# Later chunks of seven norms read an operand already scaled by the norm, and more weight chunks take wide products

## The chip, the cores and the metric

The kernel runs on 1 core of one Trainium2 chip. The metric is the device time of one execution in microseconds (us), the median of the runs shown. The profile is one further execution of the same program. The core has five engines that run side by side: TensorE (PE; its weight loads are shown apart as PEld), VectorE (DVE), ScalarE (ACT), GpSimd (POOL) and SyncE (SP), which issues the loads of the weights. Each engine takes its own instructions strictly in the order of the program, and they wait for one another on semaphores.

## The reference, cut to what matters

The program is four transformer blocks on one sequence of 256 tokens and width 1024: two of a first kind, then two layers of a second kind.

```python
# first kind, twice (the mixer differs)
h = h + mixer(rms_norm(h, mix_norm_g[l]))
h = h + conv_ffn(rms_norm(h, ffn_norm_g[l]), ...)     # conv of the 2*3072 columns, u * gelu(g), down

# second kind, two layers
h = swiglu(rms_norm_2(x, ffn1_pre[l]), w_gate_up, w_down)        # 2*2816 columns
x = x + 0.5 * rms_norm_2(h, ffn1_post[l])
z = rms_norm_2(x, mix_pre[l]) @ w_in                             # b_g, c_g, v, p, gates
y_a = (b_g * causal_depthwise_conv(c_g * v, conv_w)) @ w_conv_out
y_p = pool_mixer(p, ...) @ w_pool_out                            # trailing means over 2, 4, 8, 16
x = x + rms_norm_2((g_a * y_a + g_p * y_p) @ w_o, mix_post[l])
h = swiglu(rms_norm_2(x, ffn2_pre[l]), ...)                      # like the first
```

A norm is `x * 1/rms(x) * gain`. All matrices are float32.

## The kernel before

The activations stand with the 1024 channels in 8 tiles of 128 partitions and the 256 tokens along the free side. The weights, 313 chunks of 1 MB (128 partitions x 16 blocks of 128 columns), are streamed once. A chunk is two output tiles (256 output channels) for 8 input tiles.

**Split products.** Every operand is split in two float32r parts, a high one and the rest. ACT makes the high part of a chunk (`w_hi`, L234), DVE the rest (`w_lo`, L243, a subtraction of 128x2048), and PE sums high x high, high x low and low x high. There are 3 buffers for raw chunks (`RAWS`) and 4 for split ones (`RING`): while DVE and ACT treat chunk n, ACT splits chunk n + 4 and DVE makes the rest of chunk n + 3. SP issues the load of chunk n + 3 when the rest of chunk n is made.

**Narrow and wide chunks.** `multiply` (L261 to L263) takes 48 matmuls for a chunk: 8 input tiles x 2 output tiles x 3 products of 256 columns. Its two output tiles share one PSUM bank. `multiply_wide` (L277, L282) puts the high and the low part of the activation side by side into one matmul of 512 columns, which leaves 32: 16 of 512 columns and 16 of 256. Its output tiles take a whole bank each, and their right halves (the high x low product) must be added to the left ones. ACT copies the right halves out (L781) and DVE adds them (L324). The rotation through the PSUM banks has `BANKS` = 4. A narrow chunk takes one of them and a wide chunk two. PE may start a chunk when DVE has taken the last user of its banks (semaphore `pair_taken`): a narrow chunk waits for the take of the chunk 4 before it, a wide one among wide ones for the take of the chunk 2 before it.

Before the change the wide chunks are the down projections and, of the gated expansions `upA` and `upB` of the second kind, the chunks from the 6th (`NARROW` = 5) on, 17 in each.

**Norms.** The mean of squares that a norm needs comes late. So the chunks after a norm multiply `x * gain` (the tile `x_split`, split by L420 and L425), and DVE multiplies each result by the reciprocal `inv_rms` when it takes it from PSUM (`take_scaled`, L330; for a wide chunk it is a second operation, L327). `inverse_spread` (L368) makes that reciprocal at the second chunk. After a post norm of the second kind, x itself has still to be divided by that norm's rms: DVE makes the reciprocal in `unroot_dve` (L382) and POOL multiplies x by it in place, 4 operations in `residual_pool` (L393).

**The stages around the change.** `up_dve`, `up_act` and `up_pool` treat the results of an expansion, chunk by chunk. In `up0` and `up1` (24 chunks each, first kind) DVE takes a chunk, makes a rest (L243), and does 4 convolution taps (L831), and POOL does two operations (L881, L887). In `upA` and `upB` (22 chunks) the activation needs no taps. `hybrid_dve`, `hybrid_act` and `pool_means` treat the mixer's input projection: 4 chunks `bg`, 4 `pool_in`, 8 `cv`, 8 `gates`. In `bg` chunk 3 DVE runs `unroot_dve` for the norm before. In `pool_in` chunk g DVE takes the chunk, makes a rest (L243), waits for ACT's high part of the pooled difference g - 1, subtracts (L1753), and sums the windows (L1781, L1782). POOL makes the mean and the difference of chunk g from these windows (L1745, L1748), ACT rounds the difference (L1368), and so on for the next g. POOL's first mean stands in its queue behind its 4 operations on x.

## Time and profile before

| what | us |
|---|---|
| median of 3 runs | 1861.85 (1861.85 to 1862.13) |
| the profiled execution: time | 1861.95 |
| the profiled execution: span | 1860.1 |
| PE busy, of the span | 1822.5 |
| DVE busy | 1436.2 |
| ACT busy | 972.5 |
| POOL busy | 204.1 |

The span runs from the first instruction to the end of the last; the rest of the time lies around it. Matmuls are pipelined, so the busy time of a group of them adds overlapping instructions only once, while a single matmul's duration is far longer than the distance from its start to the next one's. The distance between starts is what a matmul costs in a full stream.

### The profile page before, as it was taken

The page shows a single profiled execution, that of the slowest core. Times are in us where ns is not written, and L with a number is a line of the kernel's source. Part 1 is how long each engine was busy: PE and PEld are TensorE (multiplying, and loading weights), DVE is VectorE, ACT ScalarE, POOL GpSimd, SP SyncE. Part 2 cuts the span into 40 slices and gives each one's busy share as a digit, 9 for nine tenths or more (in the row PEclk, how much of TensorE's full clock was granted, in tenths as well). Part 3 has the DMA queues.
Part 4 walks back from the last instruction along what each step waited for, and adds up shares of the span by engine and source line. Part 5 has one row for each costly group of instructions (what it writes and reads, how often), then busy time and mean ns, then how long its engine had stood idle before and what let it go on. Part 6 is the DMA issues. An engine that isn't in the chain of part 4 may idle for free.

```text
span 1860.1 us, 31793 instructions
## 1 busy us (share of the span) xinstructions
PE 1822.5 (98%) x13284; PEld 1720.6 (92%) x13284; DVE 1436.2 (77%) x1707; ACT 972.5 (52%) x1174; POOL 204.1 (11%) x160
## 2 busy tenths in 40 slices
PE   7999999999999999999999999999999999999997
PEld 7889999999999998899999998889888999999887
DVE  7987996598998578758875797759775896578774
ACT  6356665385765455544453555545553445445542
POOL 2001321000432030002200010001000320001000
PEclk9999999999999999999999999999999999999999
DMA  7324555434555545564454455554555445445551
GB/s 291 131 105 159 184 183 201 182 137 181 182 204 181 204 159 183 204 221 146 164 199 175 159 188 197 192 193 167 196 204 204 159 174 191 157 161 205 199 207 67
DMA packets 46789, 334.67 MB, mean 180 GB/s; under 512 B 5184, under 2 KB 5568, under 8 KB 6464
## 3 DMA queue, kind: packets, MB, share of 16 engines
q1 hardware_dynamic: 46512, 332.20, 49.3%
q8 instruction: 105, 1.72, 0.4%
q0 software_dynamic: 144, 0.52, 0.1%
q14 instruction: 28, 0.23, 0.0%
HBM read 331.65 MB, written 1.05 MB: 179 GB/s over the span
## 4 chain that ended last, share of the span: by engine, by line
PE 82%; DVE 10%; ACT 3%; POOL 2%; DMA 1%; issue 1%; SPq 0%; DVEq 0%; ACTq 0%
PE psum L277 24%; PE psum L282 12%; PE psum L261 11%; PE psum L263 11%; PE psum L262 11%; PE psum L303 6%; DVE w_lo L243 4%; PE psum L310 3%; POOL scratch L1748 1%; DMA w_raw<-stream_in 1%; POOL x_resid L393 1%; ACT w_hi L234 1%; POOL scratch L1745 1%; DVE scratch L330 1%; PE psum L599 1%
## 5 line engine op out<-in xcount | busy, mean ns | idle before, releaser
L234 ACT ACTIVATE w_hi<-w_raw 128x2048 fp32r<-128x2048 f32 x313 | 597.3, 1913 | 416.3 <-PE psum L263 157.6
L243 DVE TENSOR_TENSOR w_lo<-w_raw,w_hi 128x2048 fp32r<-128x2048 f32 x313 | 724.1, 2316 | 37.8 <-ACT w_hi L234 37.7
L261 PE MATMUL psum<-x_split,w_hi 128*128 128x256 f32 x1896 | 541.0, 285 | 13.9 <-DVE x_split L425 10.5
L262 PE MATMUL psum<-x_split,w_hi 128*128 128x256 f32 x1896 | 537.0, 283 | 0.0
L263 PE MATMUL psum<-x_split,w_lo 128*128 128x256 f32 x1896 | 537.0, 283 | 0.0
L261 PEld LDWEIGHTS psum<-x_split,w_hi 128*128 128x128 f32 x1896 | 364.4, 192 | 15.4 <-issue 14.8
L262 PEld LDWEIGHTS psum<-x_split,w_hi 128*128 128x128 f32 x1896 | 364.5, 192 | 0.5
L263 PEld LDWEIGHTS psum<-x_split,w_lo 128*128 128x128 f32 x1896 | 364.4, 192 | 0.0
L277 PE MATMUL psum<-x_split,w_hi 128*128 128x512 f32 x1088 | 341.7, 395 | 0.0
L277 PE MATMUL psum<-h_split,w_hi 128*128 128x512 f32 x816 | 256.3, 395 | 0.0
L282 PEld LDWEIGHTS psum<-x_split,w_lo 128*128 128x128 f32 x1088 | 204.4, 188 | 48.3
L282 PE MATMUL psum<-x_split,w_lo 128*128 128x256 f32 x1088 | 213.7, 278 | 0.0
L282 PEld LDWEIGHTS psum<-h_split,w_lo 128*128 128x128 f32 x816 | 153.3, 188 | 36.2
L277 PEld LDWEIGHTS psum<-x_split,w_hi 128*128 128x128 f32 x1088 | 165.6, 189 | 0.0
L282 PE MATMUL psum<-h_split,w_lo 128*128 128x256 f32 x816 | 160.3, 278 | 0.0
L393 POOL TENSOR_TENSOR x_resid<-x_resid,squares 128x512 f32<-128x512 f32 x24 | 45.4, 1923 | 902.6 <-DVE squares L382 902.5
L261 PE MATMUL psum<-h_split,w_hi 128*128 128x256 f32 x480 | 136.1, 283 | 1.3 <-ACT scratch L1298 0.7
L262 PE MATMUL psum<-h_split,w_hi 128*128 128x256 f32 x480 | 135.8, 283 | 0.0
L263 PE MATMUL psum<-h_split,w_lo 128*128 128x256 f32 x480 | 135.8, 283 | 0.0
L330 DVE TENSOR_TENSOR scratch<-psum,inv_rms 128x512 f32<-128x512 f32 x137 | 92.7, 683 | 43.3 <-PE psum L263 42.8
L277 PEld LDWEIGHTS psum<-h_split,w_hi 128*128 128x128 f32 x816 | 124.2, 189 | 0.0
L781 ACT ACTIVATE scratch<-psum 128x512 f32<-128x512 f32 x68 | 40.6, 598 | 158.5 <-PE psum L282 158.5
(249 smaller groups left out, 2412.3 us busy)
## 6 DMA issues: line engine op xcount, KB each, us to landing
w_raw<-stream_in SPq DMA_DIRECT2D x313, 1024.0 KB, 4.8
x_resid<-x_in SPq DMA_DIRECT2D x1, 1024.0 KB, 7.1
y_out<-x_resid SPq DMA_DIRECT2D x4, 256.0 KB, 2.5
scratch<-mask_in SPq DMA_DIRECT2D x1, 768.0 KB, 11.1
scratch<-ev_in SPq DMA_DIRECT2D x1, 512.0 KB, 9.7
scratch<-inv_in POOLq DMA_DIRECT2D x1, 512.0 KB, 6.6
params<-par_in SPq DMA_DIRECT2D x1, 247.0 KB, 7.3
matrices<-mat_in SPq DMA_DIRECT2D x1, 192.0 KB, 8.9
```

The costliest lines, as they stand in the source:

```text
L234: act.activation(w_hi[:, n % RING, :], raw[:, n % RAWS, :], ACT.Copy).then_inc(hi_ready, 1)
L243: dve.tensor_tensor(w_lo[:, n % RING, :], raw[:, n % RAWS, :], w_hi[:, n % RING, :].bitcast(F32), ALU.subtract).then_inc(lo_ready, 1)
L261: pe.matmul(dst, w_hi[:, c.slot, b:b + P], src[:, k0 + k, 0, :], start=opens, stop=False)
L262: pe.matmul(dst, w_hi[:, c.slot, b:b + P], src[:, k0 + k, 1, :], start=False, stop=False)
L263: done = pe.matmul(dst, w_lo[:, c.slot, b:b + P], src[:, k0 + k, 0, :], start=False, stop=last and k == nk - 1 and m == len(tiles_) - 1)
L277: pe.matmul(ps[:, bank_, :], w_hi[:, c.slot, b:b + P], src[:, k0 + k, :, :].rearrange("p a t -> p (a t)"), start=first and k == 0, stop=False)
L282: done = pe.matmul(tile(bank_, 0), w_lo[:, c.slot, b:b + P], src[:, k0 + k, 0, :], start=False, stop=last and k == nk - 1)
L303: pe.matmul(tile(c.bank, m), w[:, c.slot, b:b + P], src[:, k0 + k, 0, :], start=k == 0 and m == 0 and w is w_hi, stop=False)
L310: done = pe.matmul(tile(c.bank, m), w_hi[:, c.slot, b:b + P], src[:, k0 + k, 1, :], start=False, stop=k == nk - 1 and m == 1)
L330: dve.tensor_tensor(dst, bank(c.bank, tiles), rinv[:, :].unsqueeze(1).to_broadcast([P, tiles, T]), ALU.mult).then_inc(pair_taken, 1)
L393: pool.tensor_tensor(x[:, 2 * g:2 * g + 2, :], x[:, 2 * g:2 * g + 2, :], UNRMS.unsqueeze(1).to_broadcast([P, 2, T]), ALU.mult).then_inc(*t ...
L781: act.activation(S(ACC + 2 * c.slot, 2), ps[:, c.bank:c.bank + 2, T:2 * T], ACT.Copy)\
```

## The change

1. `WIDE` and `SCALED` say for each stage from which chunk on it is wide, and from which it is scaled. Wide are now also: `up0` and `up1` from chunk 7 (17 chunks each), `pool_in` chunk 3, all 8 `cv` and all 8 `gates` chunks of both layers. `upB` is wide from chunk 6 and not from 5. `upA` stays.
2. A scaled chunk (all the newly wide ones, and `upA` and `upB` from chunk 7) multiplies another operand, x times the gain times the reciprocal. DVE makes it with 8 operations (`scale_dve`), ACT rounds it with 4 (`scaled_hi`) and DVE makes the rest with 4 (`scaled_lo`). Its result needs no second multiplication. There are eight of these operands in an execution.
3. In an expansion, DVE makes the operand behind chunks 2 and 3 and the rests behind chunks 4 and 5, each the last of its chunk. In the mixer, it makes the operand behind `bg` chunk 2 and the rests behind `bg` chunk 3.
4. `unroot_dve` stands behind these: in `upA` and `upB` at chunk 5 and not 3, in the mixer still at `bg` chunk 3, but after the rests.
5. PE waits, in a scaled chunk, for rest k // 2 + 1 before input tile k.

```diff
-WIDE = ("upA", "upB")
+WIDE = {"up0": 7, "up1": 7, "upA": 5, "upB": 6, "pool_in": 3, "cv": 0, "gates": 0}
+SCALED = {"up0": 7, "up1": 7, "upA": 7, "upB": 7, "pool_in": 3, "cv": 0, "gates": 0}
...
         def take_scaled(dve, c, dst, tiles=2):
             dve.wait_ge(chunk_done, c.number + 1)
             if c.wide:
-                dve.wait_ge(up_right, wide_count(c))
-                dve.tensor_tensor(dst, ps[:, c.bank:c.bank + 2, 0:T], S(ACC + 2 * c.slot, 2),
+                dve.wait_ge(up_right, WIDE_COUNT[c.number])
+                dve.tensor_tensor(dst, ps[:, c.bank:c.bank + 2, 0:T], right_halves(c),
                                   ALU.add).then_inc(pair_taken, 2)
+                if c.scaled:
+                    return
...
+        def copy_right(act, c):
+            act.activation(right_halves(c), ps[:, c.bank:c.bank + 2, T:2 * T], ACT.Copy).then_inc(up_right, 1)
...
+        def scale_dve(dve, tr, phase, gain, ks):
+            for k in ks:
+                dve.scalar_tensor_tensor(out=scaled_words(phase)[:, k, 1, :], in0=x[:, k, :],
+                                         scalar=gain[:, k:k + 1], in1=rinv[:, :],
+                                         op0=ALU.mult, op1=ALU.mult).then_inc(*tr["xn"].one())
+
+        def scaled_hi(act, tr, phase, gs, l):
+            for g in gs:
+                act.wait_ge(*tr["xn"].count(2 * g + 2, l))
+                act.activation(scaled_operand(phase)[:, 2 * g:2 * g + 2, 0, :],
+                               scaled_words(phase)[:, 2 * g:2 * g + 2, 1, :], ACT.Copy)\
+                   .then_inc(*tr["xhi"].one())
+
+        def scaled_lo(dve, tr, phase, gs, l):
+            for g in gs:
+                dve.wait_ge(*tr["xhi"].count(g + 1, l))
+                both = scaled_operand(phase)[:, 2 * g:2 * g + 2, :, :]
+                dve.tensor_tensor(both[:, :, 1, :], scaled_words(phase)[:, 2 * g:2 * g + 2, 1, :],
+                                  both[:, :, 0, :].bitcast(F32), ALU.subtract).then_inc(*tr["xlo"].one())
...
+            if c.scaled:
+                multiply_wide(pe, c, (c.bank, c.bank + 1), scaled_operand(c.phase), 0, KT, True, True,
+                              lambda k: tr["xlo"].count(k // 2 + 1, c.layer), hooks=hooks)
...
# up_act
+                if phase in SCALED and at in (3, 4):
+                    scaled_hi(act, pre, phase, (0, 1) if at == 3 else (2, 3), l)
...
# up_dve
-                    if at == 3 and post is not None:
-                        unroot_dve(dve, *post)
+                if phase in SCALED and at in (2, 3):
+                    scale_dve(dve, pre, phase, gain, range(0, 4) if at == 2 else range(4, 8))
+                if phase in SCALED and at in (4, 5):
+                    scaled_lo(dve, pre, phase, (0, 1) if at == 4 else (2, 3), l)
+                if at == 5 and post is not None:
+                    unroot_dve(dve, *post)
...
# hybrid_act
                 refill_hi(act, c)
+                if g == 2:
+                    scaled_hi(act, N["normM"], "pool_in", G4, l)
...
                 act.wait_ge(chunk_done, c.number + 1)
+                if c.wide:
+                    copy_right(act, c)
                 refill_hi(act, c)
...
# hybrid_dve
                 refill_lo(dve, c)
+                if g == 2:
+                    scale_dve(dve, N["normM"], "pool_in", gains2("mpre", l), range(KT))
                 if g == 3:
+                    scaled_lo(dve, N["normM"], "pool_in", G4, l)
                     unroot_dve(dve, PN["postA"], l)
```

## Rows read from the trace of the kernel before

**Rows 1.** The page: busy time of each engine.

```profile
PE 1822.5 (98%) x13284; PEld 1720.6 (92%) x13284; DVE 1436.2 (77%) x1707; ACT 972.5 (52%) x1174; POOL 204.1 (11%) x160
```

**Rows 2.** Stages up0, up1: length, busy PE, PEld, DVE, ACT, POOL, clock.

```profile
165.40:291.40 126.00, 126.00 (x1051) 125.96 (x1051) 121.78 (x139) 82.10 (x115) 42.01 (x43) 1.00 0.53 187
459.60:585.60 126.00, 126.00 (x1050) 125.96 (x1050) 121.33 (x139) 83.80 (x116) 43.82 (x43) 1.00 0.51 183
```

**Rows 3.** Timeline of PE: first matmuls of two successive chunks, narrow, then wide.

```profile
1529.81 0.28 PE L261 MATMUL psum<-x_split,w_hi 128*128 128x256 f32 x1
...
1535.57 0.28 PE L261 MATMUL psum<-x_split,w_hi 128*128 128x256 f32 x1
...
779.80 0.40 PE L277 MATMUL psum<-h_split,w_hi 128*128 128x512 f32 x1
...
785.38 0.40 PE L277 MATMUL psum<-h_split,w_hi 128*128 128x512 f32 x1
```

**Rows 4.** Timeline of PE in layer 0's mixer: cv chunk 3 starts.

```profile
907.65 0.36 PE L261 MATMUL psum<-x_split,w_hi 128*128 128x256 f32 x1 [1.24 <-DVE w_lo L243]
```

**Rows 5.** Timeline of DVE in layer 0's mixer, bg chunk 2 to cv chunk 1.

```profile
847.05 3.25 DVE L425 SCALAR_TENSOR_TENSOR x_split<-x_resid,params,x_split 128x256 fp32r<-128x256 f32 x8
...
869.59 1.74 DVE L382 RECIPROCAL squares<-squares 128x256 f32<-128x256 f32 x1
...
884.40 0.69 DVE L1753 TENSOR_TENSOR h_split<-scratch,h_split 128x512 fp32r<-128x512 f32 x1 [3.21 <-ACT h_split L1368]
...
907.43 1.50 DVE L1814 TENSOR_TENSOR scratch<-scratch 128x256 f32<-128x256 f32 x1
909.35 0.69 DVE L1753 TENSOR_TENSOR h_split<-scratch,h_split 128x512 fp32r<-128x512 f32 x1 [0.42 <-ACT h_split L1368]
909.96 0.69 DVE L330 TENSOR_TENSOR scratch<-psum,inv_rms 128x512 f32<-128x512 f32 x1
...
914.47 0.69 DVE L330 TENSOR_TENSOR scratch<-psum,inv_rms 128x512 f32<-128x512 f32 x1
```

**Rows 6.** Timeline of POOL in the same stretch.

```profile
871.41 7.63 POOL L393 TENSOR_TENSOR x_resid<-x_resid,squares 128x512 f32<-128x512 f32 x4 [169.51 <-DVE squares L382]
878.99 3.35 POOL L1745 TENSOR_TENSOR scratch<-scratch 128x512 f32<-128x512 f32 x1
882.41 1.29 POOL L1748 TENSOR_TENSOR scratch<-scratch 128x512 f32<-128x512 f32 x1
```

**Rows 7.** Timeline of DVE: four rests of 128x512.

```profile
428.36 2.49 DVE L1721 TENSOR_TENSOR h_split<-scratch,h_split 128x512 fp32r<-128x512 f32 x4
```

**Rows 8.** Timeline of DVE: takes of chunks 3 and 5 in up0, of 3 in up1.

```profile
178.60 0.68 DVE L330 TENSOR_TENSOR scratch<-psum,inv_rms 128x512 f32<-128x512 f32 x1
179.21 2.28 DVE L243 TENSOR_TENSOR w_lo<-w_raw,w_hi 128x2048 fp32r<-128x2048 f32 x1
182.86 2.65 DVE L831 SCALAR_TENSOR_TENSOR scratch<-scratch,params 128x255 f32<-128x255 f32 x4 [1.38 <-ACT scratch L773]
...
190.79 0.68 DVE L330 TENSOR_TENSOR scratch<-psum,inv_rms 128x512 f32<-128x512 f32 x1
...
473.98 0.68 DVE L330 TENSOR_TENSOR scratch<-psum,inv_rms 128x512 f32<-128x512 f32 x1
```

**Rows 9.** Timeline of PE: chunk 7 of up0 and of up1 starts.

```profile
193.18 0.28 PE L261 MATMUL psum<-x_split,w_hi 128*128 128x256 f32 x1
...
487.27 0.28 PE L261 MATMUL psum<-x_split,w_hi 128*128 128x256 f32 x1
```

**Rows 10.** ACT's copies of right halves, all of them.

```profile
L781 ACT ACTIVATE scratch<-psum 128x512 f32<-128x512 f32 x68 | 40.6, 598 | 158.5 <-PE psum L282 158.5
```

**Rows 11.** Loads of chunks: count, size, us from issue to landing.

```profile
w_raw<-stream_in SPq DMA_DIRECT2D x313, 1024.0 KB, 4.8
```

**Rows 12.** The clock: two of PE's first matmuls, and a stretch behind its last.

```profile
12.98 0.41 PE L263 MATMUL psum<-x_split,w_lo 128*128 128x256 f32 x1
13.19 0.41 PE L261 MATMUL psum<-x_split,w_hi 128*128 128x256 f32 x1
...
1853.00:1856.00 3.00, 0.00 (x0) 0.00 (x0) 2.93 (x7) 0.00 (x0) 0.00 (x0) 0.55 0.46 175
```

More of the change, by code:

```diff
@@ L98 @@
 EV_GK, EV_Q = 2, 3
-PRE, ACC, GEL, HID, HB = 0, 8, 16, 20, 24
+PRE, ACC, GEL, HID, HB, XN = 0, 8, 16, 20, 24, 24
+HYBRID = ("bg", "pool_in", "cv", "gates")
+SCALED_NORMS = ["ffnnorm0", "ffnnorm1", "normA", "normM", "normB"]
 YA, PIN, GA, GP, PRE2, ACC2, UU, INV = 0, 8, 16, 24, 32, 38, 41, 44
@@ L157, in __init__ @@
         self.slot = self.number % RING
-        self.wide = phase in WIDE and n >= NARROW
-        self.event = E0[phase] + n + layer * LAYER_EVENTS + (n - NARROW if self.wide else 0)
+        self.wide = phase in WIDE and n >= WIDE[phase]
+        self.scaled = phase in SCALED and n >= SCALED[phase]
+        self.event = E0[phase] + n + layer * LAYER_EVENTS + (n - WIDE[phase] if self.wide else 0)
         self.bank = self.event % BANKS
+        assert not self.wide or self.bank % 2 == 0, phase
         self.last = self.event + 1 if self.wide else self.event
@@ L167, in chunks @@
     return [Chunk(phase, n, layer) for n in range(done, count)]
+WIDE_COUNT, UNSCALED_COUNT = {}, {}
+_w, _u = 0, 0
+for _layer, _stages in [(0, FIRST)] + [(_l, LAYER) for _l in range(LAYERS2)]:
+    for _name, _nc, _ in _stages:
+        for _n in range(_nc):
+            _chunk = Chunk(_name, _n, _layer)
+            _w += _chunk.wide
+            _u += _chunk.wide and not _chunk.scaled
+            WIDE_COUNT[_chunk.number], UNSCALED_COUNT[_chunk.number] = _w, _u
 def program(nc, x_in, stream, par1_in, par2_in, ev_const, mask_const, mats, inv_in, out):
@@ L743, in up_tracks @@
             return {k: Signal(sem(f"{name}_{k}_ready"), 2 * m if k == "taps" else m) for k in names}
-        def wide_count(c):
-            return (WIDE.index(c.phase) + 2 * c.layer) * (FF2 - NARROW) + c.n - NARROW + 1
         def scaled(c):
-            if c.wide:
-                return up_scaled, wide_count(c)
-            return taken(c.event)
+            if c.wide and not c.scaled:
+                return up_scaled, UNSCALED_COUNT[c.number]
+            return taken(c.last)
         def up_act(act, phase, n, tr, func, conv, pre, l, final=None):
@@ L769, in taps @@
                 w, b = conv
-                act.wait_ge(*taken(c.event))
+                act.wait_ge(*taken(c.last))
                 for t in range(2):
@@ L1410, in hybrid_act @@
                 act.wait_ge(chunk_done, c.number + 1)
+                copy_right(act, c)
                 refill_hi(act, c)
-                act.wait_ge(*taken(c.event))
+                act.wait_ge(*taken(c.last))
                 for t, dst in enumerate((GA, GP)):
@@ L1775, in hybrid_dve @@
                     pooled_lo(g - 1)
-                dve.wait_ge(*taken(c.event))
+                dve.wait_ge(*taken(c.last))
                 src = S(PIN + 2 * g, 2)
```

62 lines of the change are left out of this document (40 added, 22 removed).

## The prediction

> **What bounds the kernel now.** I read the page first: PE is busy for 98% of the span, DVE for 77%, ACT for half, POOL for a tenth [rows 1]. So a shorter stream of matmuls is worth its whole length, but only where nothing else comes last. The busy time of stages says where DVE is close behind: in up0 it is busy for 121.78 of 126.00 us and in up1 for 121.33 of 126.00, with PE never idle [rows 2]. The waits of PE and its timeline then show the one stall that comes in both mixers: cv chunk 3 starts at 907.65 after 1.24 us of idling that a weight rest of DVE ends [rows 4]; it is the same at 1507.08 in layer 1. The timelines of DVE and POOL there show what makes DVE late. DVE's reciprocal at 869.59 lets POOL work on x from 871.41 for 7.63 us; then POOL makes the first mean and difference, and DVE gets them at 884.40 after 3.21 us of idling [rows 5, 6]. From there DVE, POOL and ACT hand a loop on: DVE's four subtractions L1753 run from 884.40 to 909.35, and the rest of cv chunk 3 is done at 907.43, between the last two [rows 5]. That is when PE goes on. So in the mixer the start of that reciprocal sets PE's time, and there is no slack in it.
>
> **What a wide chunk gives.** A narrow chunk takes 1535.57 - 1529.81 = 5.76 us, a wide one 785.38 - 779.80 = 5.58 us [rows 3], though both stream the same number of columns. That is 0.18 us for each. Newly wide are 17 + 17 chunks of up0 and up1 and 1 + 8 + 8 in each mixer, 34; each upB loses one. Net 66 chunks, 11.9 us at most.
>
> The Trainium skill (TensorE: Matmul & The Clock Gate, "Back-to-back issue gap") speaks against the change: it gives a start-to-start gap of columns / 2.4 plus about 2.5 ns. By it a chunk is 48 x 109.2 ns = 5.24 us narrow and 16 x (215.8 + 109.2) ns = 5.20 us wide, and 66 chunks an estimated 2.6 us and not 11.9. The rows show 120 ns for each narrow matmul, so I go by them.
>
> **What each newly wide chunk costs elsewhere.** ACT copies the right halves, 0.60 us [rows 10]; with 82 to 84 us busy in 126 [rows 2] it has room for 17 of them (10 us). DVE's take is an addition in place of a multiplication, taken as equal. The 60 chunks of upA and upB that are now scaled lose DVE's second operation. DVE has slack there, so this gives nothing. The cost that counts is that only two wide chunks fit into the PSUM banks, so DVE's take of the chunk before the last must be done when a chunk starts; until now it was the fourth before.
>
> **The new operand.** Eight operations of DVE of 128x256 with a scalar: 3.2 us, 0.40 each, as the eight of the same form that split x took 3.25 [rows 5]. Four rests of 128x512: 2.4 us, 0.60 each, as the four of that form took 2.49, of which the last's end overlaps the next operation [rows 7]. ACT's four rounds run beside. Together DVE gets 5.6 us of work, eight times. Where that is hidden it costs nothing:
>
> *upA, upB.* DVE has no taps there. I followed the work through chunks 2 to 5: the last two rests end about 1.5 us or more before PE needs them in chunk 7. The later unroot_dve starts POOL's work on x two chunks later, and the next reader of x comes only after the down projection. Cost 0; POOL slows DVE while it works, at worst some 0.7 us in upA of layer 1. Each upB is 0.18 slower, 0.4 in all.
>
> *up0.* DVE's take of chunk 3 stands at 178.60. Four scalings come before it (1.6 us), and DVE's idle 1.38 us at 182.86, a wait for ACT, absorbs them or, if ACT is also pushed back, doesn't. Four more scalings (1.6) and two rests (1.2) move the take of chunk 5 from 190.79 [rows 8] to 190.79 + 1.6 - 1.4 + 1.6 + 1.2 = 193.8, or 195.2. Behind it are the take (0.6), a weight rest (2.2), taps (2.6) [rows 8] and only then the third rest of the operand (0.6): ready at 199.8 to 201.2. PE starts chunk 7 at 193.18 [rows 9]; with 4 input tiles behind it (2.8 us) it needs that rest at 196.0. It waits 3.8 to 5.2 us. I take 4.4.
>
> *up1.* The same, but DVE stands at 473.98 where it stood at 178.60, 295.4 later [rows 8], and PE at 487.27 where it was at 193.18, only 294.1 later [rows 9]. It waits 1.3 longer, 5.1 to 6.5 us; I take 5.7.
>
> After this DVE gains on PE: its chunk is 0.6 + 2.2 + 2.6 = 5.4 us against 5.58. So one stall in each. Sum of up0 and up1: 4.4 + 5.7 - 34 x 0.18 = +4.0 us.
>
> *The mixer.* The eight scalings and four rests all stand between bg chunk 2 and the reciprocal, and DVE works without a pause there. The reciprocal moves from 869.59 to 875.2, POOL's start from 871.41 to 877.0 [rows 5, 6]. POOL's 7.63 us then end at 884.6, inside a weight rest that slows both (as at 878.99, 3.35 us for an operation that takes 1.29 alone) [rows 6]. DVE's first subtraction goes from 884.40 to 889.3 or, with the last operation on x caught too, 890.1. The loop from there took 24.95 us to the fourth (884.40 to 909.35) and is the same. So the fourth is at 914.3 to 915.1, and the take of cv chunk 1, which stands right behind it, ends 1.2 us later, 915.5 to 916.3. Until now nobody waited for that take. Now cv chunk 3 needs its banks: it starts at 915.5 to 916.3 and not at 907.65 [rows 4], 7.9 to 8.7 us later. I take 8.3. PE meets the same hold at cv chunks 0, 1 and 2, with some 3 us of idling each, all contained in this figure, as are the shorter pool_in 3 to cv 2. Left to gain are 13 wide chunks (cv 3 to 7, gates), 2.3 us; DVE's 914.47 - 909.96 = 4.5 us for a cv chunk, or 4.9 with a rest of the convolution in it, is short of 5.58. Each mixer +6.0, both +12.0.
>
> *Loads.* SP issues the load of chunk n + 3 behind the rest of chunk n, so loads move with DVE. A load lands in 4.8 us [rows 11], and it has three chunks of 5.6 less ACT's split and DVE's rest; nothing waits for it.
>
> **The clock.** PE's first matmuls come 0.21 us apart where the later ones come 0.12 apart, and behind the last matmul, at 1850.8, the granted clock falls from 1.00 (2.4 GHz) to a mean of 0.55 in the stretch 1853 to 1856 [rows 12], so the lower level is 0.5 (1.2 GHz). From the first matmul at 10.5 to the rise at about 13.4 us are 14 matmuls at 0.09 more each, 1.3 us. No gap inside the kernel is longer than 1.7 us and none lowers the clock, so the new gaps of 3 to 6 us are outside what the trace shows: 0 to 1.3 us each, eight of them. I take one, for the longest. The Trainium skill (the same page, "What's actually happening") says that an idle array is put back to half the clock. It says nothing about the price here.
>
> **The sum.** +4.0 + 12.0 + 0.4 + 1.3 = +17.7 us. From 1861.95, the time of the profiled execution (0.1 above the median of the runs): 1879.6 us, 0.95% slower. Its own range: up stages 2.8 to 5.6, mixers 11.2 to 12.8, clock 0 to 5, upA up to 0.7: 1876 to 1886.
>
> **The rivals.**
> - *Only the mixers stall.* If the rests of the operand come in time in up0 and up1 (DVE finds 5 us of pauses more than I see), these gain 6.1: 1861.95 + 12.0 + 0.4 - 6.1 = 1868.3. For: with PE at 98%, DVE's idle time is hard to place. Against: 4.2 us of it in 126, and the need comes at chunk 7.
> - *Faster: DVE's extra work is hidden everywhere.* That needs a reciprocal in bg chunk 3 on which PE's stall doesn't hang, and a DVE that catches up before chunk 7. Then 66 x 0.18 come off: 1850. It decides from the point where all added stalls are together below 11.9 us. For: DVE idles 3.21 us at 884.40. Against: that idling is a wait for the very loop that the reciprocal starts.
> - *Only up0 and up1 stall.* The mixer's stalls stay as now and it gains 17 x 0.18 twice: 1861.95 + 4.0 + 0.4 + 1.3 - 6.1 = 1861.6, no change.
> - *The clock falls in every gap.* Seven more times 1.3: 1888.7. Against: in the mixer PE waits for POOL anyway, and a slower chunk is partly hidden by the next wait.
> - *The old wait stays the last.* If the two banks don't bind, cv chunk 3 waits only for its weight rest, 4.9 to 5.7 later: 1879.6 - 6 = 1873.6. It lies in the range.
>
> **Chances.** My sum with its near variants (the last rival too) 0.73; only mixers 0.10; hidden everywhere 0.08; only up stages 0.04; clock everywhere 0.05. The range 1867 to 1888 leaves out the second and third of these other cases and the top of the last. A measurement of this kernel can tell about 0.2% (3.7 us) from no change. Faster 0.09, within 0.2% 0.04, slower 0.87.
>
> **What would show it.** In the profile after: fewer matmuls by 66 x 16 = 1056; chunks 5.58 us apart in up0, up1, cv and gates; in both mixers L382 some 5.6 us later after the start of its stage; PE waits of about 3 us at cv 0, 1, 2 that end with DVE's take, not with w_lo; cv chunk 3 some 8 us late; in up0 and up1 one wait each inside chunk 7, released by a DVE rest of the scaled operand; no stall in upA and upB. If PE's waits in up0 and up1 are missing, the forecast is 8 to 10 us too high; if L382 isn't late or cv 3 doesn't follow it, 12 to 16 too high, and the sign can turn.

## The result, and the profile after

The changed kernel takes 1889.7 us (median of 4 runs, 1887.06 to 1892.69) against 1861.99 us of the kernel before (4 runs, 1861.85 to 1863.18). The ratio is 1.0148, with a 95% interval of 1.013 to 1.0165: 1.5% slower. The forecast was 1879.6 us with a range of 1867 to 1888. The sign and the places were right, the loss was 28.8 us (profiled executions, 1861.95 to 1890.76) in place of 17.7, and the time lies 1.7 us above the range. Of all runs shown below one, of the kernel that is wide only where DVE keeps up, took 2528.9 us at a mean granted clock of 0.655; its median and ratio leave it out. The title counts seven norms; the scaled operands are eight in an execution, as the change says.

The page of the changed kernel begins with its span and the busy time of each engine, to be read against [rows 1]:

```profile
span 1889.0 us, 29813 instructions
PE 1826.4 (97%) x12228; PEld 1673.2 (89%) x12228; DVE 1439.2 (76%) x1741; ACT 1020.4 (54%) x1272; POOL 206.4 (11%) x160
```

There are 13284 - 12228 = 1056 fewer matmuls, as forecast, and yet PE is busy for 3.9 us longer: a part of the new matmuls ran slowly. The waits of PE hold three entries of several us that the kernel before did not have, all on lines of the wide chunk. Each gives the line that waits, the engine and line waited for, the us in total, how many times, and the longest:

```profile
PE psum L304 <- DVE scaled_split L399: 11.0, 4, 3.4
PE psum L304 <- DVE scratch L351: 9.9, 7, 3.2
PE psum L304 <- DVE scratch L359: 7.6, 2, 3.8
```

L399 is the rest of the scaled operand, L351 and L359 are DVE's takes of wide and of narrow chunks. Lines have moved: L243 of before is L270 (rest of a weight), L330 is L359, L324 is L351, L382 is L454 (the reciprocal), L393 is L465 (POOL on x), L1745 is L1828, L1753 is L1836.

The timeline of PE shows where these waits lie. Its columns are start and duration in us, the instruction, and in brackets the idling before it with what ended it. First come the two in up0, then three of cv in layer 0:

```profile
194.56 0.71 PE L304 MATMUL psum<-scaled_split,w_hi 128*128 128x512 f32 x2 [1.44 <-DVE scaled_split L399]
201.00 1.22 PE L304 MATMUL psum<-scaled_split,w_hi 128*128 128x512 f32 x2 [3.42 <-DVE scaled_split L399]
...
903.39 1.22 PE L304 MATMUL psum<-h_split,w_hi 128*128 128x512 f32 x2 [3.83 <-DVE scratch L359]
911.68 0.73 PE L304 MATMUL psum<-h_split,w_hi 128*128 128x512 f32 x2 [1.14 <-DVE scratch L351]
920.77 1.22 PE L304 MATMUL psum<-h_split,w_hi 128*128 128x512 f32 x2 [3.23 <-DVE scratch L351]
```

Two such matmuls take 0.71 to 0.73 us behind a short wait and 1.22 us behind a wait of over 3 us. The windows of those stretches (start and end, length, busy PE, PEld, DVE, ACT, POOL, granted clock, share of the DMA engines, GB/s) say why:

```profile
199.70:206.50 6.80, 5.50 (x17) 4.72 (x18) 6.80 (x10) 1.71 (x4) 2.14 (x2) 0.50 0.47 163
500.10:506.90 6.80, 5.83 (x18) 4.96 (x19) 6.80 (x9) 2.01 (x5) 2.14 (x2) 0.50 0.48 175
902.90:906.30 3.40, 2.90 (x9) 2.52 (x10) 3.34 (x2) 0.00 (x0) 3.32 (x2) 0.50 0.00 0
919.90:926.70 6.80, 5.93 (x18) 5.06 (x19) 6.38 (x7) 1.92 (x3) 4.48 (x2) 0.50 0.26 87
```

In each the granted clock is 0.50, the 1.2 GHz level. In these four it begins while PE is still idle: from 199.7 where PE goes on at 201.00, from 902.9 where it goes on at 903.39. There are two more, of 3.4 us each, from 1513.8 and 1530.9, which begin 0.6 and 0.3 us after PE goes on. The kernel before has none from its rise at about 13.5 us until PE's work is over.

The table gives the length of each stage, worked out as the difference between the ends of the last matmuls of successive stages in the timeline of PE.

| stage | before, us | after, us | difference |
|---|---|---|---|
| up0 | 139.34 | 144.05 | +4.71 |
| up1 | 138.66 | 144.76 | +6.10 |
| pool_in, each layer | 23.04 | 22.85 | -0.19 |
| cv of layer 0, of layer 1 | 47.55, 47.53 | 57.64, 56.45 | +10.09, +8.92 |
| gates, each layer | 46.08 | 44.59 | -1.49 |
| upA of layer 0, of layer 1 | 124.39, 127.62 | 124.39, 128.99 | 0, +1.37 |
| upB of layer 0, of layer 1 | 128.02, 128.09 | 128.70, 128.66 | +0.68, +0.57 |
| the first stage | | | -0.2 |
| all others | | | 0 |

These add up to 28.9 us, the whole difference within rounding.

DVE in layer 0's mixer, to be read against [rows 5], from the new scalings to the fourth subtraction:

```profile
877.41 3.25 DVE L382 SCALAR_TENSOR_TENSOR h_spare<-x_resid,params,inv_rms 128x256 f32<-128x256 f32 x8
...
883.38 2.49 DVE L399 TENSOR_TENSOR h_split<-h_spare,h_split 128x512 fp32r<-128x512 f32 x4
885.79 1.75 DVE L454 RECIPROCAL squares<-squares 128x256 f32<-128x256 f32 x1
...
900.59 0.69 DVE L1836 TENSOR_TENSOR h_split<-scratch,h_split 128x512 fp32r<-128x512 f32 x1 [4.46 <-ACT h_split L1445]
...
920.03 0.68 DVE L351 TENSOR_TENSOR scratch<-psum,scratch 128x512 f32<-128x512 f32 x1
...
925.44 0.69 DVE L1836 TENSOR_TENSOR h_split<-scratch,h_split 128x512 fp32r<-128x512 f32 x1 [0.41 <-ACT h_split L1445]
```

And POOL in the same stretch, against [rows 6]:

```profile
887.61 9.66 POOL L465 TENSOR_TENSOR x_resid<-x_resid,squares 128x512 f32<-128x512 f32 x4 [159.30 <-DVE squares L454]
897.23 1.29 POOL L1828 TENSOR_TENSOR scratch<-scratch 128x512 f32<-128x512 f32 x1
```

Compare distances from the end of the stage bg, which is at 866.10 before and 876.72 after. The reciprocal is 3.49 us behind it before and 9.07 after. The first subtraction is at 18.30 and 23.87, the fourth at 43.25 and 48.72. So all three are 5.5 to 5.6 us later, about the length of the inserted work (3.25 + 2.49 less overlaps), and nothing between absorbs it. POOL's part is longer on x and shorter on the first mean, 7.63 + 3.35 before and 9.66 + 1.29 after: 10.98 and 10.95 us, the same.

### The profile page after: what moved, and what is told of

Its sections match the earlier page's. It is cut to its first block, busy times and chain, and to the rows that moved or that the text cites. A ratio compares the mean times of both kernels' runs of the same rounds, so it can differ in the third digit from the quotient of the medians.

```text
span 1889.0 us, 29813 instructions
## 1 busy us (share of the span) xinstructions
PE 1826.4 (97%) x12228; PEld 1673.2 (89%) x12228; DVE 1439.2 (76%) x1741; ACT 1020.4 (54%) x1272; POOL 206.4 (11%) x160
## 4 chain that ended last, share of the span: by engine, by line
PE 73%; DVE 19%; ACT 3%; POOL 3%; issue 1%; DMA 1%; SPq 0%; DVEq 0%; ACTq 0%; POOLq 0%
PE psum L304 34%; PE psum L309 17%; DVE w_lo L270 6%; PE psum L330 6%; PE psum L288 3%; PE psum L290 3%; PE psum L289 3%; PE psum L337 3%; DVE scratch L359 1%; POOL x_resid L465 1%; DVE scratch L904 1%; POOL scratch L1831 1%; ACT w_hi L261 1%; DVE scratch L382 1%; DVE inv_rms L440 1%
## 5 line engine op out<-in xcount | busy, mean ns | idle before, releaser
L270 DVE TENSOR_TENSOR w_lo<-w_raw,w_hi 128x2048 fp32r<-128x2048 f32 x313 | 726.2, 2322 | 37.7 <-ACT w_hi L261 37.6
L304 PE MATMUL psum<-scaled_split,w_hi 128*128 128x512 f32 x1504 | 476.9, 399 | 12.4 <-DVE scaled_split L399 11.0
L304 PE MATMUL psum<-h_split,w_hi 128*128 128x512 f32 x1360 | 433.0, 400 | 16.1 <-DVE scratch L351 8.5
L309 PEld LDWEIGHTS psum<-scaled_split,w_lo 128*128 128x128 f32 x1504 | 284.9, 189 | 67.7
L309 PE MATMUL psum<-scaled_split,w_lo 128*128 128x256 f32 x1504 | 297.3, 279 | 0.0
L309 PE MATMUL psum<-h_split,w_lo 128*128 128x256 f32 x1360 | 270.0, 280 | 0.0
L288 PE MATMUL psum<-x_split,w_hi 128*128 128x256 f32 x840 | 242.5, 289 | 10.4 <-DVE x_split L497 10.4
L304 PEld LDWEIGHTS psum<-scaled_split,w_hi 128*128 128x128 f32 x1504 | 231.2, 190 | 13.8 <-DVE scaled_split L399 7.2
L289 PE MATMUL psum<-x_split,w_hi 128*128 128x256 f32 x840 | 238.6, 284 | 0.0
L290 PE MATMUL psum<-x_split,w_lo 128*128 128x256 f32 x840 | 238.5, 284 | 0.0
L351 DVE TENSOR_TENSOR scratch<-psum,scratch 128x512 f32<-128x512 f32 x134 | 92.4, 690 | 142.6 <-ACT scratch L368 138.3
L288 PEld LDWEIGHTS psum<-x_split,w_hi 128*128 128x128 f32 x840 | 162.1, 193 | 11.4 <-issue 10.7
L289 PEld LDWEIGHTS psum<-x_split,w_hi 128*128 128x128 f32 x840 | 162.2, 193 | 0.5
L290 PEld LDWEIGHTS psum<-x_split,w_lo 128*128 128x128 f32 x840 | 162.1, 193 | 0.0
L465 POOL TENSOR_TENSOR x_resid<-x_resid,squares 128x512 f32<-128x512 f32 x24 | 49.8, 2105 | 916.1 <-DVE squares L454 916.0
L290 PE MATMUL psum<-h_split,w_lo 128*128 128x256 f32 x480 | 135.8, 283 | 0.0
```

Of the source, the lines that this page charges most:

```text
L270: dve.tensor_tensor(w_lo[:, n % RING, :], raw[:, n % RAWS, :], w_hi[:, n % RING, :].bitcast(F32), ALU.subtract).then_inc(lo_ready, 1)
L288: pe.matmul(dst, w_hi[:, c.slot, b:b + P], src[:, k0 + k, 0, :], start=opens, stop=False)
L289: pe.matmul(dst, w_hi[:, c.slot, b:b + P], src[:, k0 + k, 1, :], start=False, stop=False)
L290: done = pe.matmul(dst, w_lo[:, c.slot, b:b + P], src[:, k0 + k, 0, :], start=False, stop=last and k == nk - 1 and m == len(tiles_) - 1)
L304: pe.matmul(ps[:, bank_, :], w_hi[:, c.slot, b:b + P], src[:, k0 + k, :, :].rearrange("p a t -> p (a t)"), start=first and k == 0, stop=False)
L309: done = pe.matmul(tile(bank_, 0), w_lo[:, c.slot, b:b + P], src[:, k0 + k, 0, :], start=False, stop=last and k == nk - 1)
```

## The experiments

Each diff is against the changed kernel. Where a fill of idle time is tried, the filler matmuls write to a bank that is never read and compute nothing.

**Operand later in up0 and up1.** The two up stages turn wide and scaled at chunk 9.

```diff
-WIDE = {"up0": 7, "up1": 7, ...
-SCALED = {"up0": 7, "up1": 7, ...
+WIDE = {"up0": 9, "up1": 9, ...
+SCALED = {"up0": 9, "up1": 9, ...
```

> The changed kernel with up0 and up1 wide and scaled from chunk 9 and not from chunk 7; the operand is made at the same places. Theory (PE waits in chunk 7 because the third rest of the operand comes at the end of DVE's chunk 5, and the idling then lowers the clock): the operand is ready when chunk 9 starts, both waits in each stage go (1.6 + 3.6 us in up0, 2.9 + 3.6 in up1) and no stretch of low clock is left there. Each stage is then 15 x 0.185 = 2.8 us shorter than in the kernel before, 136.5 us for up0 and 135.9 for up1, and the whole about 1889.7 - 16.5 = 1873. Rival (DVE with its taps can't keep the pace of wide chunks, 5.4 us against 5.58 plus the wait for ACT's copy; chunk 7 is only where it shows first): the wait moves to chunk 9 or 10, at least 2 us of it stay in each stage, and the whole stays over 1880.

Measured: 1883.8 us (1882.71 to 1884.88), ratio 1.0116 (1.0086 to 1.0145). up0 is 1.77 us longer than before and up1 3.03. The waits for L399 went, but another took their place at the second wide chunk, as the rival had it. The timelines of PE and DVE in this kernel show it:

```profile
213.11 0.73 PE L304 MATMUL psum<-scaled_split,w_hi 128*128 128x512 f32 x2 [2.62 <-DVE scratch L359]
```

```profile
212.38 0.68 DVE L359 TENSOR_TENSOR scratch<-psum,inv_rms 128x512 f32<-128x512 f32 x1
```

Chunk 10 needs the banks of chunk 8, and DVE takes chunk 8 about 7.7 us behind PE. While chunks are narrow DVE may be that late; with two wide chunks in the banks it may be about 5 us late. (The 5 us are an estimate: the wide chunk between lasts 5.58 us, and the take itself 0.68.) So behind the operand's own lateness lies a second cause, DVE's lag, and moving the change by two chunks only swaps the wait. The clock fell to 0.5 for 3.4 us in each stage here too, behind idling of 2.62 us.

**Fillers in up0 and up1.** 6 matmuls ahead of chunk 7 and 14 ahead of its fifth input tile keep PE at work through the idling.

```diff
+        def filler_pe(pe, n):
+            for k in range(n):
+                pe.matmul(ps[:, 7, :], xs[:, k % KT, 0, 0:P], ...
...
+                if c.phase in ("up0", "up1") and c.n == 7:
+                    filler_pe(pe, 6)
+                    hooks = {3: lambda: filler_pe(pe, 14)}
```

> The changed kernel with matmuls of 512 columns that compute nothing (into an idle PSUM bank) in the waits of chunk 7 of up0 and up1: 6 before the chunk, 14 before its input tile 4, about 0.23 us each. Nothing else is changed. Theory (the low clock is a separate cost of about 2.7 us in each of the two stages, caused by the idling): the granted clock stays at 1.00 through both stages, DVE's rests come at the same times, and each stage is 2 to 3 us shorter than in the changed kernel (up0 144.05 to 141 or 142, up1 144.76 to 142), the whole about 5 us. Rival (the low clock costs nothing by itself, because PE would wait for DVE anyway, and the matmuls are only in the way): both stages as long as in the changed kernel or longer.

Measured: 1885.0 us (1884.34 to 1885.66), ratio 1.0122 (1.0093 to 1.0152). up0 takes 141.57 us and up1 142.15, with no low clock in either; chunk 7 of up0 takes 10.97 us and not 13.37. The clock alone cost 144.05 - 141.57 = 2.5 us and 144.76 - 142.15 = 2.6 us. The run with POOL's order changed, below, bears this out without a filler: no low stretch fell in its up0, and that took 141.56 us. More work on PE made the kernel faster.

**Fillers in the mixers.** 14, 4 and 12 of the same ahead of cv chunks 0, 1 and 2.

```diff
+                if ph == "cv" and c.n < 3:
+                    filler_pe(pe, (14, 4, 12)[c.n])
                 pe.wait_ge(pair_taken, c.last + 1)
```

> The changed kernel with matmuls that compute nothing in the mixer's waits: 14 before cv chunk 0, 4 before chunk 1, 12 before chunk 2, in both layers, about 0.23 us each. Theory (of the two or three stretches of low clock only the one in which cv chunk 2 itself runs slowly costs time, since the chunks before it have to wait for DVE anyway): in layer 0 the stage cv goes from 57.6 to 54.7 us, in layer 1, where the low stretch after chunk 2's wait is shorter, from 56.5 to about 55, the whole about 4 us less. Rival (the loop of POOL and DVE holds everything, the clock nothing): cv stays at 57.6 and 56.5. Second rival: each stretch of low clock costs its full 1.3 us and more, the whole is 8 us less.

Measured: 1885.52 us (1885.37 to 1885.67), ratio 1.0125 (1.0096 to 1.0154). cv takes 55.40 us in both layers, against 57.64 and 56.45. The same window of layer 0 with (first fence, this kernel) and without fillers (second fence, the changed kernel):

```profile
895.00:930.00 35.00, 32.15 (x171) 26.58 (x170) 27.08 (x37) 14.71 (x16) 16.24 (x9) 1.00 0.40 137
```

```profile
895.00:930.00 35.00, 26.81 (x128) 22.77 (x127) 26.19 (x35) 12.21 (x14) 18.27 (x9) 0.85 0.35 124
```

The mean granted clock is 1.00 in place of 0.85. At full clock, cv chunk 3 starts 50.1 us behind the end of bg, where it was 41.55 before: 8.6 later, where 8.3 was forecast. The starts of cv chunks 0, 1 and 2 in layer 0 are 26.7, 35.0 and 44.1 us behind the end of bg with and without the fillers. So a low stretch that is followed by another wait cost nothing here. Only chunk 3, which starts behind the last wait, moves: 52.5 to 50.1 us in layer 0 and 51.3 to 50.1 in layer 1.

Of the 5.4 us between the profiled executions of the two kernels, 2.2 lie in up0 and up1, which the edit does not touch: the low clock fell otherwise there (for 3.4 us in up0, and twice for 3.4 in up1, with 6.8 at once in each in the changed kernel). So where one kernel is set against another here, the stage lengths say more than the whole times.

**Fillers in both.** The two edits before, together.

> The changed kernel with the matmuls that compute nothing in both places, up0 and up1 as in the one run and the mixer as in the other. Theory (the low clock costs 8.3 us of the changed kernel's time, 2.4 + 2.6 in up0 and up1, 2.2 + 1.1 in the mixers, and the waits the rest): the granted clock is 1.00 to the end of the last matmuls, and the time is 1889.7 - 8.3 = 1881.4, within 1.5 us; the repeats agree better than those of the changed kernel (1887.1 to 1892.7). Rival (the low clock comes from elsewhere and would fall anyway): low stretches stay, and the time is over 1885.

Measured: 1883.23 us (1882.55 to 1883.9), ratio 1.0115 (1.0071 to 1.0158). up0 takes 141.57 us, up1 142.17, cv 55.42 and 55.38: the two effects add. The whole is 0.3 us above the range that was expected. Its profiled execution has a low stretch where neither the change nor the fillers touch the code. Near 123 us, in the attention stage, the clock fell for 3.4 us and that stage took 40.95 us in place of 39.31:

```profile
120.00:130.00 10.00, 8.94 (x70) 7.74 (x70) 4.57 (x7) 4.88 (x6) 0.00 (x0) 0.83 0.01 2
```

Less those 1.6 us its profiled execution is at 1882.3, 8.5 us below the changed kernel's 1890.8.

**The mixer's 17 chunks wide without an operand.** The rest stays as in the changed kernel. The scaling of the 17 chunks is done at their take, as in the other unscaled wide chunks, and the reciprocal stands where it stood before.

```diff
-SCALED = {"up0": 7, "up1": 7, "upA": 7, "upB": 7, "pool_in": 3, "cv": 0, "gates": 0}
+SCALED = {"up0": 7, "up1": 7, "upA": 7, "upB": 7}
...
-                if g == 2:
-                    scale_dve(dve, N["normM"], "pool_in", gains2("mpre", l), range(KT))
                 if g == 3:
-                    scaled_lo(dve, N["normM"], "pool_in", G4, l)
                     unroot_dve(dve, PN["postA"], l)
```

> The changed kernel without the mixer's scaled operand: the same 17 mixer chunks are wide, but they multiply x times the gain, as upA does from chunk 5, and DVE multiplies each by the reciprocal in a second operation (0.6 us). The eight scalings and four rests of the mixer are gone, and unroot_dve stands where it stood in the kernel before. Theory (5.6 us of DVE's work ahead of unroot_dve set the loop back, and the two PSUM banks make PE wait for it): the first subtraction is back at 18.3 us after bg chunk 3 is done and not 23.9. Some stall is left, since PE still waits for the take of cv chunk 1 where it used to wait for nothing, and three takes have a second operation: cv chunk 3 starts 3.5 to 5.5 us later than in the kernel before. Stage cv 49 to 51 us (47.5 before, 57.6 changed), the whole 12 to 16 us below the changed kernel. Rival (the two-bank hold alone makes the stall, the operand's work is hidden): cv stays over 55 us.

Measured: 1880.94 us (1880.90 to 1880.98), ratio 1.0101 (1.0071 to 1.013). cv takes 49.71 us in both layers and no clock falls there. So 5.7 of the 7.9 us by which cv grew at full clock are the operand's, and 2.2 stay: the two banks bind also without it. Chunks 1 and 2 of cv wait 1.0 and 3.0 us for a take, and no low stretch follows the longer one. gates take 46.80, 2.2 more than in the changed kernel, since PE idles 1.9 us ahead of gates chunk 2; that DVE is still behind there because of the second operation of its take is argued, not shown. All of these are in the waits for the wide take:

```profile
PE psum L304 <- DVE scratch L351: 13.9, 11, 3.0
```

The whole is 8.8 us below the changed kernel, and not 12 to 16: the expectation held for cv and missed the gates.

**The operand is made, and not used.** The mixer's DVE and ACT do all the new work, but its 17 chunks stay narrow and read the old operand. upB is wide from chunk 5 again.

```diff
-WIDE = {"up0": 7, "up1": 7, "upA": 5, "upB": 6, "pool_in": 3, "cv": 0, "gates": 0}
-SCALED = {"up0": 7, "up1": 7, "upA": 7, "upB": 7, "pool_in": 3, "cv": 0, "gates": 0}
+WIDE = {"up0": 7, "up1": 7, "upA": 5, "upB": 5}
+SCALED = {"up0": 7, "up1": 7, "upA": 7, "upB": 7}
```

> The changed kernel with the mixer's 17 chunks narrow again (and upB wide from chunk 5). The mixer's scaled operand is still made at the same places, but no matmul reads it: the work of DVE and ACT for it alone. Theory (it is this work ahead of unroot_dve that sets the loop of DVE, POOL and ACT back, whether the chunks are wide or not): unroot_dve starts 5.6 to 5.7 us later than in the kernel before, and cv chunk 3 starts 5 to 6 us later, released by its weight rest as before: stage cv 52.5 to 53.5 us against 47.5, gates as before. Rival (the two-bank hold of the wide chunks alone makes the stall): cv 47.5 to 48.

Measured: 1890.55 us (a single run, so no ratio). The reciprocal is 9.08 us behind the end of bg, as in the changed kernel. cv takes 54.39 and 53.08 us, 6.8 and 5.5 more than before, though not one chunk is wide. The whole is no shorter than the changed kernel, since gates and pool_in lose what the width gave (3.4 us), the two upB take 1.4 more, and this execution too has the low stretch near 123 us (1.6). The waits in cv now end with a weight rest, as the one in [rows 4] did:

```profile
908.05 0.36 PE L288 MATMUL psum<-x_split,w_hi 128*128 128x256 f32 x1 [0.91 <-DVE w_lo L270]
...
916.35 0.36 PE L288 MATMUL psum<-x_split,w_hi 128*128 128x256 f32 x1 [2.33 <-DVE w_lo L270]
...
925.42 0.55 PE L288 MATMUL psum<-x_split,w_hi 128*128 128x256 f32 x1 [3.09 <-DVE w_lo L270]
```

Chunk 3 starts 47.1 us behind the end of bg in both layers. In layer 0 a low stretch of 3.4 us begins at 925.0, behind the last wait; in layer 1 one of the same length begins at 1525.7, ahead of the last wait. The first costs the 1.3 us by which the two stages differ, the second nothing. Read together with the run before it, at full clock: the operand's 5.6 us of DVE cost 5.5 to 5.7 us in each mixer's cv with or without wide chunks, and the banks cost another 2.2 to 2.3, net of the 1.5 that eight wide chunks give.

**POOL's means ahead of its work on x.** If the loop is what sets PE's time, then an earlier start of the loop must come off cv.

```diff
             for l in range(LAYERS2):
-                residual_pool(pool, PN["postA"], l)
                 pool_means(pool, l)
+                residual_pool(pool, PN["postA"], l)
```

> The changed kernel with one exchange in POOL's queue: in the mixer, the means and differences of the pooling come first and the four operations on x behind them. Theory (POOL's work on x, released by the late unroot_dve, stands in front of the first mean and keeps DVE's first subtraction waiting): the first subtraction comes about 3 us earlier after the end of bg, cv chunk 3 starts 3 us earlier, and less time is spent at the low clock: stage cv 51.5 to 54.5 us in layer 0 against 57.6, the whole 6 to 12 us below 1889.7. Rival (POOL's work on x isn't in the chain, DVE's own lag after the scalings is): cv over 56.5 us in both layers.

Measured: 1880.32 us (1879.38 to 1881.25), ratio 1.0097 (1.0077 to 1.0117). POOL makes the first mean at once, released by DVE's scratch and no longer behind the work on x:

```profile
887.46 1.29 POOL L1828 TENSOR_TENSOR scratch<-scratch 128x512 f32<-128x512 f32 x1 [162.41 <-DVE scratch L1868]
```

The first subtraction is 19.58 us behind the end of bg and not 23.87, 4.3 earlier; cv takes 53.30 and 53.26, 4.3 and 3.2 less. Part of that is the clock. Against the run with fillers, cv chunk 3 starts 3.2 and 3.7 us earlier (46.9 and 46.4 us behind the end of bg, and not 50.1), and cv is 2.1 us shorter. So this part of the chain is on the path, for most of its 4.3 us. The rest is lost again ahead of cv chunk 4, where PE now idles 0.95 us in layer 0 and 1.29 in layer 1. POOL's work on x lies beside DVE's takes there:

```profile
1532.07 0.50 PE L304 MATMUL psum<-h_split,w_hi 128*128 128x512 f32 x1 [1.29 <-DVE scratch L351]
```

```profile
1522.25 7.89 POOL L465 TENSOR_TENSOR x_resid<-x_resid,squares 128x512 f32<-128x512 f32 x4
```

Of the 11.4 us between the profiled executions of the two kernels, 3.6 lie in up0 and up1, where the low clock fell otherwise.

**The reciprocal of upA and upB later.** It stands behind chunk 12 and not behind chunk 5.

```diff
-                if at == 5 and post is not None:
+                if at == 12 and post is not None:
                     unroot_dve(dve, *post)
```

> The changed kernel with unroot_dve of upA and upB behind chunk 12 and not behind chunk 5. Theory (the small stalls at chunk 9 of upA in layer 1 and of both upB come from POOL's four operations on x, which the change puts where DVE is still behind and which slow DVE's weight rest from 2.3 to 3.4 us and two small operations from 0.4 to 1.5): at chunk 12 DVE has room, and upA of layer 1 goes from 128.99 back to 127.6, each upB from 128.7 to about 128.2 (the one chunk less that is wide stays, 0.2). Rival (the scalings and rests alone make DVE late there): the stages stay at 129.0 and 128.7.

Measured: 1884.96 us (a single run, so the whole says little; the stage lengths are what to read). upA of layer 1 takes 127.62 us, exactly what it took before, and the two upB 128.21 and 128.18. Of the 2.6 us that these stages lost, all but 0.3 (about the one chunk that each upB has fewer) came from POOL's work on x, which the reciprocal starts and which lay beside the first scaled chunks. In the changed kernel POOL and DVE there look like this:

```profile
1316.25 7.72 POOL L465 TENSOR_TENSOR x_resid<-x_resid,squares 128x512 f32<-128x512 f32 x4 [183.07 <-DVE squares L454]
```

```profile
1307.14 0.42 DVE L888 TENSOR_TENSOR scratch<-scratch 128x256 f32<-128x256 f32 x1
...
1316.09 0.63 DVE L351 TENSOR_TENSOR scratch<-psum,scratch 128x512 f32<-128x512 f32 x1
1316.75 1.34 DVE L356 TENSOR_TENSOR scratch<-scratch,inv_rms 128x512 f32<-128x512 f32 x1
1318.01 3.38 DVE L270 TENSOR_TENSOR w_lo<-w_raw,w_hi 128x2048 fp32r<-128x2048 f32 x1
1321.31 1.51 DVE L888 TENSOR_TENSOR scratch<-scratch 128x256 f32<-128x256 f32 x1
```

The same small operation takes 0.42 us alone and 1.51 beside POOL, the weight rest 3.38 and not 2.28, and PE then idles for 1.09 us at 1324.91.

**Wide only where DVE keeps up.** up0 and up1 turn wide and scaled at chunk 17, gates turn wide at chunk 1 without an operand, the reciprocals stand at their old places, and pool_in and cv are narrow.

```diff
-WIDE = {"up0": 7, "up1": 7, "upA": 5, "upB": 6, "pool_in": 3, "cv": 0, "gates": 0}
-SCALED = {"up0": 7, "up1": 7, "upA": 7, "upB": 7, "pool_in": 3, "cv": 0, "gates": 0}
+WIDE = {"up0": 17, "up1": 17, "upA": 5, "upB": 6, "gates": 1}
+SCALED = {"up0": 17, "up1": 17}
```

> Wide chunks only where DVE is no longer behind: up0 and up1 wide and scaled from chunk 17 (operand made behind chunks 2 to 5 as in the change), gates wide from chunk 1 but not scaled, pool_in and cv narrow, upA and upB not scaled (upB wide from 6), unroot_dve where it stood in the kernel before. Theory (a wide chunk gives its 0.185 us only if DVE is less than about 5 us behind PE; DVE recovers 0.41 us with each narrow chunk and is near 7.7 at chunk 8): no stall is added anywhere; up0 and up1 are 1.3 us shorter each, gates 1.3 in each layer, each upB 0.2 longer: 4.8 us in all, 1857. Rival (the scaled operand's 5.6 us of DVE work in up0 and up1 cost something by themselves): a stall of 2 us or more stays in up0 and up1, and the whole is at 1860 or over.

Measured: 1858.45 us (median of nine runs, 1858.22 to 1861.16), ratio to the kernel before 0.9982 (0.9972 to 0.9992): 0.2% faster, a little short of the 1857 expected. up0 is 1.17 us shorter than before, gates 1.31 each. up1 gains nothing (+0.07): its narrow chunks 8 and 9 start 0.5 and 0.8 us late, after 0.36 and 0.56 us of idling that a weight rest of DVE ends. DVE is 1.3 us further behind there from the start, as [rows 8, 9] had it. So the making of the operand alone costs nothing in up0 and 1.4 us in up1.

**The same with POOL's order changed.** The edit is the last two shown here together.

> The same as the kernel with late wide chunks, with POOL's order in the mixer exchanged too (means and differences first, then x). Theory: the 1.24 us stall at cv chunk 3 goes or shrinks to below 0.5 in both layers, since DVE's first subtraction comes 1 to 2 us earlier: 1.5 to 2.5 us less than without the exchange, about 1855. Rival (the loop's length and not its start sets that stall, since a turn takes 7.5 to 9.1 us against chunks of 5.76): less than 0.5 us is gained.

Measured: 1856.3 us (1855.25 to 1858.4, 8 runs), ratio 0.9968 (0.9958 to 0.9979). This is 0.3% faster than the kernel before, and the fastest of all shown. cv takes 46.08 us, exactly 8 narrow chunks of 5.76: the stall of [rows 4], which was in the kernel before, is gone in both layers. The waits of PE for a weight rest, without and with the new order:

```profile
PE psum L288 <- DVE w_lo L270: 3.9, 5, 1.2
```

```profile
PE psum L288 <- DVE w_lo L270: 0.9, 2, 0.6
```

The two that are left are those of up1.

## Why the prediction was right, and where it failed

The sum, term by term. "At full clock" is with fillers or, for the others, where no stretch of the lower clock lies in the stage.

| term | forecast, us | measured, us | miss |
|---|---|---|---|
| up0 and up1 at full clock | +4.0 | +5.7 | +1.7 |
| two mixers at full clock | +12.0 | +12.4 | +0.4 |
| upA and upB | +0.4 | +2.6 | +2.2 |
| clock | +1.3 | +8.4 | +7.1 |
| first stage | 0 | -0.2 | -0.2 |
| sum | +17.7 | +28.9 | +11.2 |

**What a wide chunk gives** was right: pool_in is 0.19 us shorter for its one, gates 1.49 for eight, 0.185 each. The estimate by the Trainium skill (TensorE: Matmul & The Clock Gate, "Back-to-back issue gap") was 0.04. The section gives that formula for an isolated matmul, and says that in a stream the weight loads count too; here each matmul has its own weight load (PEld x12228 for PE x12228).

**The mixer** was right step by step. The reciprocal is 5.6 us late, the first subtraction 5.6 (forecast 4.9 to 5.7), the fourth 5.5, and cv chunk 3 is 8.6 late at full clock where 8.3 was taken. PE's waits at cv 0 to 2 end with takes, L359 and L351, and not with w_lo; two of them are over 3 us, as forecast, and the one at cv 1 is 1.1 us and less. The run with POOL's order changed shows that this loop is on the path, and the run with the unused operand shows that the DVE work alone delays it by 5.5 us. The rival in which the old wait stays the last is out: with it cv chunk 3 would start 5.5 us later, as it does with narrow chunks, and not 8.6.

**up0 and up1** waited inside chunk 7 and for L399, as it was said, but twice and not once. The first wait, 1.44 us in up0 and 2.70 in up1, stands ahead of the chunk's first input tile. By the prediction's own times the first rest ends at 193.2 to 194.6 (its take of chunk 5 less one rest of 0.6), and PE needs it at 193.18; it did not count that wait. This alone costs nothing, since the third rest is waited for last. At full clock the waits are 5.4 us in up0 and 6.6 in up1 (the stage's growth plus 17 x 0.185), against 4.4 and 5.7, the middles. DVE's idling of 1.38 us was to absorb half; ACT is pushed back as well and DVE still idles 1.38 us behind the new scalings. So the later end of each range, 5.2 and 6.5, was the true one:

```profile
184.24 2.64 DVE L904 SCALAR_TENSOR_TENSOR scratch<-scratch,params 128x255 f32<-128x255 f32 x4 [1.38 <-ACT scratch L845]
```

**upA and upB** had POOL's slowing of DVE as "at worst some 0.7 us in upA of layer 1", and nothing of it in the sum. It was 1.4 there and about 0.5 more than forecast in each upB. That POOL does it is shown by the run with the later reciprocal; that the two-bank hold is what leaves DVE so little room there is argued.

**The step that failed is the clock term.** "0 to 1.3 us each, eight of them. I take one, for the longest": the mechanism is right and the size is not. Of the eight new gaps that were counted, two (cv chunk 1) were of 1.1 us or less, and the six over 3 us all had a stretch at 1.2 GHz. Four of these stretches cost time: 2.5 us in up0, 2.6 in up1, and 2.2 and 1.1 behind cv chunk 2's wait in layers 0 and 1, 8.4 in all, where 1.3 was put in the sum. In up0 a stretch of 3.4 us cost 1.3 us (from the end of chunk 6 to the end of chunk 7 it took 12.30 us with one and 10.96 with none), but one of 6.8 us cost 2.4 (13.37 us). The bound of 1.3 came from the launch [rows 12], the only stretch in the trace of before at that level; it had the price of a short stretch and not that a longer one can follow a gap. The argument that in the mixer the next wait hides a slow chunk held for the stretches at cv chunk 0, since chunk 2 starts at the same 44.1 us with and without them. It failed at chunk 2, behind which no wait comes: there the clock cost 3.3 us.

The rival in which the clock falls in every gap (1888.7 us) was nearest to the time, with 0.05. That is luck in part: four stretches cost time and not eight, two of them about twice the price, and the other misses (1.7, 0.4 and 2.2 us) came from the up stages, the mixers, upA and upB. The rivals in which a part or all of DVE's work is hidden (1868.3, 1861.6 and 1850 us) are refuted: both groups of stalls are there, each shown by its own run; no stage is shorter by its wide chunks but pool_in and gates. The clock's miss of 7.1 us alone would have left the time at 1886.7, inside the range up to 1888; the others took it out. The clock's own upper end of 5 us, in the likeliest case, was 3.4 too low.

What stays open: no run settles why the same gap of 3.4 us is followed by none, 3.4 or 6.8 us of low clock. Not tried were a reciprocal ahead of the scalings in the mixer (POOL would then overwrite x while the scalings read it) and the making of the operand on POOL.

## What to carry to other kernels

A wider product that saves 0.185 us per chunk also halves the chunks that the banks hold, so here it paid only from the point where the engine that empties them was less than a chunk behind; look for that point in the timelines of both engines, stage by stage. Work that is put ahead of a signal on which a loop over three engines hangs is paid in full (5.5 us here), though DVE was busy for 76% of the span; the same trace says which order of the signals starts that loop earlier, and that took another 2 us off the faster kernel. Price a new gap of PE of some 2.3 us or more with a slow stretch behind it (1.3 or 2.4 us more here), not with its own length alone, unless a later wait of PE absorbs it, as at cv chunk 0.

## What the runs showed of the hardware

The same idling of 3.41 to 3.42 us in up0 was met by 6.8 us of granted clock 0.5 in the changed kernel, by 3.4 us in the run with fillers in the mixers alone and by none in the run with POOL's order changed, with the same code in that stage. The wait and the window in the last of these, against the first window of the profile after:

```profile
200.96 0.50 PE L304 MATMUL psum<-scaled_split,w_hi 128*128 128x512 f32 x1 [3.41 <-DVE scaled_split L399]
```

```profile
199.70:206.50 6.80, 5.54 (x31) 4.81 (x32) 6.80 (x10) 4.11 (x6) 2.17 (x2) 1.00 0.41 160
```

Shorter gaps had one too: 2.62 us in up0 of the kernel wide from chunk 9 and 2.34 us in layer 1 of the run with the unused operand were each met by 3.4 us at 0.5, while 3.26 us ahead of cv chunk 2 in layer 1 of the run with the later reciprocal were met by none. This can account for the spread between the runs of the changed kernel (1887.06 us at a mean granted clock of 0.991 to 1892.69 at 0.989); only one of them was profiled, so it isn't shown. The Trainium skill (TensorE: Matmul & The Clock Gate, "What's actually happening") has an idle array go to half the clock; the rows agree that this is the level, and show besides that the length of a gap alone does not settle whether it comes.

In the attention stage near 123 us the clock fell for 3.4 us in three of the kernels, with no gap of PE over 0.78 us between 15 us and there; the kernel before and the changed one have none there.

DVE and POOL slow each other: while POOL works on x, DVE's operations on SBUF take 1.51 us in place of 0.42 and 3.38 in place of 2.28, and POOL's mean took 3.35 in [rows 6] and 1.29 in the changed kernel. The take that reads PSUM, at 1316.09, kept its 0.63 us beside POOL. The Trainium skill (SBUF — State Buffer, "SBUF: two separate sides") states that a DVE operation with two SBUF inputs and a GpSimd operation that reads SBUF exclude each other. The rows agree in kind.
